# Moving the context stream's front and attention of the second block into the expert phase of layer 1, with a ring of four weight slots there

## The reference, cut to what matters

```
# first block, layer i
x = x + g1 * attention(h)
y = hierarchical_moe(h, ...)       # 32 experts: silu(h @ w_gate) * (h @ w_up), then @ w_down
x = x + g2 * y
# second block, layer l
hx = rmsnorm(x) * (1 + scale) + shift ;  hy = rmsnorm(y) * (1 + scale_c) + shift_c
fy, gy, qy, ky, vy, ay = branches(hy, ...)      # h @ w_in, Fourier mix, spatial gate, q, k, v
fx, gx, qx, kx, vx, ax = branches(hx, ...)
ox = attend(qx, [ky, kx], [vy, vx]) * silu(ax)
x = x + gate * (concat(fx, gx, ox) @ w_out)
if l < 1:
    oy = attend(qy, ky, vy) * silu(ay)
    y = y + gate_c * (concat(fy, gy, oy) @ w_out)
```

## Time and profile before

| | us |
|---|---|
| median of 3 runs | 1902.62 (1901.37 to 1910.19) |
| the profiled execution | 1905.12 |
| its span | 1903.3 |
| experts of layer 1 on TensorE | 974.98 to 1483.4 |
| y's front and attention between x's fills | 1507.52 to 1606.33 |

### The profile page before, as it was taken

How to read it: one execution, slowest core, us unless ns; L and a number is a source line. 1 busy time by engine, 2 the same in 40 slices (tenths; PEclk the granted TensorE clock), 3 DMA queues, 4 the chain that set the end, 5 groups by cost and what they waited for, 6 DMA issues and landing times.

```text
span 1903.3 us, 18238 instructions
## 1 busy us (share of the span) xinstructions
PE 1696.5 (89%) x7421; PEld 845.8 (44%) x7421; DVE 489.1 (26%) x927; ACT 405.1 (21%) x909; POOL 95.9 (5%) x167
## 2 busy tenths in 40 slices
PE   5967999888988888989989999989989899889988
PEld 3823453333333334835453433433343456555564
DVE  1337230000000103244241000000102344663362
ACT  2004221111111102015131111111100334443351
POOL 1102000000000010113000000000001000100000
PEclk9988999999999999989989999999999999999999
DMA  9997269999999999987369999999999622123310
GB/s 353 389 383 283 110 267 406 421 422 422 422 423 423 423 416 400 352 349 238 132 238 421 423 416 423 418 422 417 418 419 390 238 91 89 66 80 117 115 62 23
DMA packets 122520, 586.32 MB, mean 308 GB/s; under 512 B 10290, under 2 KB 15482, under 8 KB 97848
## 3 DMA queue, kind: packets, MB, share of 16 engines
q1 hardware_dynamic: 99064, 491.94, 64.0%
q0 software_dynamic: 16192, 82.06, 11.6%
q10 hardware_dynamic: 7168, 11.02, 1.5%
HBM read 572.83 MB, written 12.15 MB: 307 GB/s over the span
## 4 chain that ended last, share of the span: by engine, by line
PE 57%; DMA 28%; DVE 7%; ACT 4%; issue 3%; SPq 1%; ACTq 0%; DVEq 0%
PE psum L2025 53%; DMA ring<-in_expert_w_up 20%; DMA work<-in_ada_w 4%; DMA ring<-in_diff_w_in 2%; DVE work L1716 1%; DMA work<-in_ctx 1%; DMA ring<-in_consts 1%; PE psum L620 1%; DVE small L967 1%; PE psum L2264 1%; PE psum L1097 1%; DVE work L1924 1%; ACT work L1639 1%; SPq L499 0%; ACT work L1503 0%
## 5 line engine op out<-in xcount | busy, mean ns | idle before, releaser
L2025 PE MATMUL psum<-ring,work 128*64 128x512 f32 (+5 forms) x4432 | 1152.0, 576 | 77.1 <-DMA ring<-in_expert_w_up 60.2
L2025 PEld LDWEIGHTS psum<-ring,work 128*64 128x64 f32 (+2 forms) x4432 | 444.4, 153 | 700.8 <-issue 668.1
L2025 PE MATMUL psum<-work 128*128 128x192 f32 (+8 forms) x920 | 193.1, 377 | 9.1 <-DVE work L1862 5.0
L1924 DVE TENSOR_TENSOR work<-work,psum 128x256 f32<-128x256 f32 x64 | 26.9, 421 | 616.5 <-ACT work L1639 616.5
L2025 PEld LDWEIGHTS psum<-work 128*128 128x128 f32 (+2 forms) x920 | 131.7, 192 | 105.1 <-issue 85.2
L1639 ACT ACTIVATE work<-psum 128x256 f32<-128x256 f32 x64 | 24.5, 383 | 691.1 <-PE psum L2025 691.1
L2025 PE MATMUL psum<-work,ring 128*128 128x256 f32 (+1 forms) x728 | 159.5, 377 | 4.5 <-DMA ring<-in_diff_w_in 1.6
L2025 PEld LDWEIGHTS psum<-work,ring 128*128 128x128 f32 x728 | 134.8, 190 | 29.2 <-issue 7.1
L1503 ACT ACTIVATE work<-psum 128x256 f32<-128x256 f32 (+4 forms) x165 | 70.3, 439 | 220.0 <-PE psum L2025 67.7
L1946 DVE TENSOR_TENSOR work<-psum,rows 128x512 f32<-128x512 f32 x64 | 44.2, 691 | 272.1 <-PE psum L2025 272.1
L1716 DVE SCALAR_TENSOR_TENSOR work<-work,small 128x2048 f32<-128x2048 f32 x28 | 65.8, 2351 | 96.4 <-DMA work<-in_ada_w 96.0
(11 more groups left out here) (256 smaller groups left out, 813.7 us busy)
## 6 DMA issues: line engine op xcount, KB each, us to landing
ring<-in_expert_w_gate SPq DMA_DIRECT2D x60, 2048.0 KB, 16.7
ring<-in_expert_w_up SPq DMA_DIRECT2D x60, 2048.0 KB, 21.3
ring<-in_expert_w_down SPq DMA_DIRECT2D x57, 2048.0 KB, 21.1
work<-in_ada_w POOLq DMA_DIRECT2D x40, 1024.0 KB, 8.5
ring<-in_w_in SPq DMA_DIRECT2D x12, 2048.0 KB, 8.8
work<-in_w_mod POOLq DMA_DIRECT2D x16, 1024.0 KB, 5.2
ring<-in_diff_w_in SPq DMA_DIRECT2D x6, 2048.0 KB, 37.5
ring<-in_sb_w_in SPq DMA_DIRECT2D x6, 2048.0 KB, 24.6
```

The lines of the kernel that those rows point to most:

```text
L1924: V.tensor_tensor(hid, s_act, gu_bank(e)[:, S:2 * S], ALU.mult).then_inc(sem("hid"), 1)
L2025: return T.matmul(out_, lhsT, rhs, start=start, stop=stop, skip_group_check=True)
```

## The change

`Y0_AT` becomes (4, 5, 6, 7, 8): y's five sections run at five experts in a row, the turns at e = 2 and 3. From e = 9 on, `y0_step` runs the 15 front steps and the 20 attention steps of y inside the experts, two per expert: one before `gate_up` (half 0, odd steps), one before `turn(hid)` (half 1, even steps). `X0_IN` is gone. From expert 7's gate on (`SPLIT`), items go round four slots; slots 4 and 5 (`KEPT`) then hold the small weights, `cst2` and y's mix and v, which GpSimd loads on its queue during the experts. Tiles of y get rooms of their own (`space_y`), banks are given out anew in layer 1 (gate_up always in bank 0, down always in bank 5), and ScalarE loads the silu table again before each expert's silu where a y step has used another. x's scores over 512 keys are two matmuls of 256 columns where they were one of 512, since y's and x's keys lie apart.

```diff
@@ ring, tables
-    Y0_AT = (6, 11, 16, 21, 26)
+    Y0_AT = (4, 5, 6, 7, 8)
+    SPLIT_AT = 7
+    SPLIT = expert_item(1, SPLIT_AT, 0)
     def slot(n):
-        return n % RING
+        return n % RING if n < SPLIT else (n - SPLIT) % (RING - KEPT)
-    X0_IN = share_steps([0, 1, 1, 1, 1, 1, 2, 2, 2, 2, 2, 3, 3, 3, 3, 3, 1, 1, 1, 1])
+    FRONT, ATTN = 15, 20
+    Y0_STEP0 = Y0_AT[-1] + 1
+    def y0_step(front, attention, e, half):
+        j = 2 * (e - Y0_STEP0) + half - 1
+        if 0 <= j < FRONT:
+            front(0, j)
+        elif FRONT <= j < FRONT + ATTN:
+            attention(0, j - FRONT)
@@ SyncE and GpSimd
-            if r == 0:
-                small_weights(sp, 0, "small_in")
-                sp.dma_start(cst2, a["consts2"]).then_inc(sem("small_in"), 16)
+                for n in range(SPLIT - RING, SPLIT):
+                    if slot(n) >= RING - KEPT:
+                        pool.wait_ge(free(n), turn_of(n) + 1)
+                small_weights(pool, 0, "small_in")
+                pool.dma_start(cst2, a["consts2"]).then_inc(sem("small_in"), 16)
@@ ScalarE, experts
+                if l:
+                    y0_step(front, attention, e, 0)
+                    if y0_roots(e):
+                        act.preload_act_table(ACT.Silu)
                 act.wait_ge(sem("gu"), EACH["gu"] * l + e + 1)
...
                 if 0 < e < TAIL:
                     store(l, e - 1)
+                if l:
+                    y0_step(front, attention, e, 1)
@@ VectorE, experts
+                    y0_step(front, attention, e, 0)
                 dve.wait_ge(sem("silu"), EACH["silu"] * l + e + 1)
...
+                if l:
+                    y0_step(front, attention, e, 1)
...
-                V.tensor_tensor(outb[:, e % 2, :], bank[5 + e % 2], gate2, ALU.mult).then_inc(sem("out_ev"), 1)
+                V.tensor_tensor(outb[:, e % 2, :], bank[down_bank(l, e)], gate2, ALU.mult).then_inc(sem("out_ev"), 1)
@@ TensorE, second block
-        for n, js in enumerate(X0_IN):
+        for n in range(2 * len(fills(1))):
             in_half(1, n)
-            for j in js:
-                front(0, j) if j < FRONT else attention(0, j - FRONT)
@@ TensorE, attention step
-                mm(bank[4 + k % 3][:, 0:n * P], qT2[...], kT2[0:A_QK, hd, 0:n * P], True, True)
+                for j in range(1 + s):
+                    ins = mm(score_bank(p, k)[:, j * S:(j + 1) * S], space(p).q[...], kT2[j][0:A_QK, hd, :], True, True)
```

More of the change, by code:

```diff
@@ L14 @@
+from collections import namedtuple
 from contextlib import ExitStack
@@ L38 @@
 RING = 6
+KEPT = 2
 SLOT = KT * 512
@@ L261, in program @@
     ACC = (1, 3, 4, 7)
-    selw = work[:, 4416:5440].rearrange("p (e t k n) -> p e t k n", e=QUAD, t=TT, k=2)
+    GATHER = (3, 1)
+    selw = [t_.rearrange("p (e t k n) -> p e t k n", e=QUAD, t=TT, k=2) for t_ in (work[:, 4416:5440], rows[:, 2, :])]
     selT = work[:, hS_at:hS_at + 1024].rearrange("p (e t q) -> p e t q", e=QUAD, t=TT)
@@ L321, in down_done, with gu_bank, down_bank, turn_of @@
         down = expert_item(l, e, 2)
-        eng.wait_ge(*((sem("early_used"), EARLY[0] * l + e + 1) if e < EARLY[l] else (free(down), down // RING + 1)))
-    def gu_bank(e):
-        return bank[0 if e >= TAIL else e % 2]
+        eng.wait_ge(*((sem("early_used"), EARLY[0] * l + e + 1) if e < EARLY[l] else (free(down), turn_of(down) + 1)))
+    SPLIT_AT = 7
+    SPLIT = expert_item(1, SPLIT_AT, 0)
+    def gu_bank(l, e):
+        return bank[0 if l or e >= TAIL else e % 2]
+    def down_bank(l, e):
+        return 5 + (0 if l and e < TAIL else e % 2)
     def slot(n):
-        return n % RING
+        return n % RING if n < SPLIT else (n - SPLIT) % (RING - KEPT)
+    def turn_of(n):
+        return sum(slot(m) == slot(n) for m in range(n))
     def loaded(eng, n):
-        eng.wait_ge(sem(f"loaded{slot(n)}"), 16 * (n // RING + (slot(n) >= 4)))
+        eng.wait_ge(sem(f"loaded{slot(n)}"), 16 * (turn_of(n) + (slot(n) >= 4)))
     def free(n):
@@ L519, in sp_second @@
         last = expert_item(1, NX - 1, 2)
-        sp.wait_ge(free(last), last // RING + 1)
+        sp.wait_ge(free(last), turn_of(last) + 1)
         for r, (p, what) in enumerate(WEIGHTS2):
@@ L852, in act_second @@
         take_turned(act, copy, 1, range(KT), (2, 3, 4, 5))
-        for n, js in enumerate(X0_IN):
-            if n % 2:
-                take_fill(act, link, copy, 1, n // 2, n // 2 % 2)
-            for j in js:
-                front(0, j) if j < FRONT else attention(0, j - FRONT)
+        for n in range(len(fills(1))):
+            take_fill(act, link, copy, 1, n, n % 2)
         c_root(act, link, 1)
@@ L1000, in dve_second @@
             stream_diag(dve, link, 1, t)
-        c_norm(dve, link, 0)
-        v_norm(dve, link, 0)
-        for n, js in enumerate(X0_IN):
-            for j in js:
-                front(0, j) if j < FRONT else attention(0, j - FRONT)
-        attention(0, 19)
         c_squares(dve, link, 1)
@@ L1336, in overflow @@
             last = expert_item(l, TAIL - 1, 2)
-            for n in range(last - RING + 1, last + 1):
-                sp.wait_ge(free(n), n // RING + 1)
+            for n in range(last - RING + l * KEPT + 1, last + 1):
+                sp.wait_ge(free(n), turn_of(n) + 1)
             for e in range(NX):
@@ L1614, in experts @@
         def experts(l):
+            front, attention = act_steps(act, link, copy)[4:]
             act.preload_act_table(ACT.Silu)
@@ L2328, in experts @@
         def experts(l):
+            front, attention = pe_steps(pe, mm)[3:]
             for e in range(NX):
                 n0, q, i = expert_item(l, e, 0), e // QUAD, e % QUAD
-                if l and e in (3, 4):
-                    if e == 4:
+                if l and e in (2, 3):
+                    if e == 3:
                         pe.wait_ge(sem("h2T"), 2)
-                    turn_stream(pe, 0, range(4 * e - 12, 4 * e - 8), Y0_BANKS)
+                    turn_stream(pe, 0, range(4 * e - 8, 4 * e - 4), Y0_BANKS)
                 if l and e in Y0_AT:
```

274 lines of the change are left out of this document (171 added, 103 removed).

## The result

The changed kernel takes 1940.0 us (median of 4 runs, 1935.2 to 1944.3) against 1902.3 us before: 1.0189 times the time, with a 95% interval of 1.0154 to 1.0224. It is 38 us slower. The forecast was 1892.5 with 1877 to 1917, so the result lies above the range.

What follows compares the result with a forecast made beforehand. Transfers bound the experts, at 15.4 us each. Terms 28 + 7.7 + 3 + 1.5 - 50.3 = -10 us on the profiled 1905.1 give 1895; the median lies 2.5 lower: 1892.5 us, range 1877 to 1917.

Steps and rivals of the forecast that it cites:

- The transfers bind the experts: Layer 1's experts: DMA needs 15.4 us per expert, TensorE 12.63 us when nothing makes it wait, so DMA decides.
- Loss A: y's sections at experts 4 to 8: TensorE binds there, hid of expert 8 comes 51.5 us late, at 1147.3.
- The transfer-bound pace of 15.4: Experts 17 to 27: with attention steps TensorE needs 14.3 us, so hids come 15.4 us apart.
- The small loads cost nothing: GpSimd's 2.8 MB fall into the DMA stall during y's sections: cost 0; uncovered they would be 7 us.
- The second block: Its start: x's fills run in one stretch, output projection starts at 1556 instead of 1606.33, a gain of 50.3 us.
- The hand-offs fit: y's steps in the experts: ScalarE's part fits by half a microsecond; rival of missing it, 1900 or 1915, chance 0.15.
- Scores in two matmuls: x's two attentions, 32 steps: same columns but one weight load more, between 0 and 5 us, 1.5 taken.
- The ring of four: Four weight slots in the experts: next up lands barely in time, 3 us taken in all.
- The margin is nil: After up lands: the next up is needed by 10.4 us, work queued ahead of it takes 10.5 us.
- The ring starves itself: Experts 9 to 27: half-clock gate_ups and late landings feed each other, up to 32 us; typically 1909, chance 0.22.
- the clock should fall less often: Experts after e = 9: TensorE's waits shrink from 2.8 us to 1, so fewer half-clock gate_ups costing 1.7 us.
- The tail: Experts 29 to 31: waits for slots add 2.8, 3.3 and 1.6 us, +7.7 us together.

Runs made afterwards that it cites:

- y5_ring5: Kernel before with y's five sections at experts 4 to 8 and five slots from expert 7 on, no step moved: 1931.2 us, ratio 1.0144.
- y5_ring4: Kernel before with y's five sections at experts 4 to 8 and four slots from expert 7 on, no step moved: 1983.7 us, ratio 1.0402.
- y5: Kernel before with only y's five sections moved to experts 4 to 8, six slots kept: 1924.8 us, ratio 1.0104.
- warm: Changed kernel plus three unused matmuls of 256 columns ahead of gate_up's wait in experts 11 to 29: 1937.4 us, ratio 1.0166.
- halves: Changed kernel, items from expert 9 loaded as two 1 MB parts, each slot part freed early, gate_up starting on first parts: 1891.4 us, again 1893.0 us.
- late: Changed kernel, from expert 10 to 29 SyncE issues the next expert's down only after the turn of hid: 1935.2 us, ratio 1.0164.

## Why the prediction was wrong

**What held.** The transfers bind the experts: yes. Loss A: `hid` of expert 8 at 1147.3 forecast, 1147.2 measured. The transfer-bound pace of 15.4 is what y5_ring5 shows, with its five slots. The small loads cost nothing: GpSimd's last one (704 KB) is issued at 1119.85 and lands 14.3 us later, at 1134.2, while TensorE first needs c at 1162.8, and the DMA engines stood at a share of 0.12 from 1105 to 1115. The second block: -50.3 forecast, -50.0 measured. The hand-offs fit: TensorE waits 1.4 us in all for ScalarE and VectorE in the experts, so that rival is out. Scores in two matmuls: the end of the traces is 36.8 us apart (1940.1 against 1903.3) and the output projection's start 32.5, of which 1.7 are its start at half clock (`turn_c` follows 34.2 us later than before, from 1616.74 to 1650.89). The remaining 2.6 us (36.8 less 34.2) hold this term, for which 1.5 was taken; it wasn't tried by itself.

**Where it failed.** The step is "The ring of four", and in it "The margin is nil ... I take 3 us in all". By the prediction's own count the term is 38 to 40 us: from `hid` 8 to 27 y5_ring4 takes 330.6 us where 19 x 15.4 are 292.6, and the changed kernel 336.3 where the prediction had 296.2, without the 3. That is 2.0 to 2.1 us per expert, mis-sized thirteenfold. (Against y5 it is 45.7 us, because the prediction's count has none of what six full slots give y5.)

Two readings in that step were wrong. The first is "Queued ahead of it are down and the next gate, 2 x 5.0, and the store 0.47: 10.5", counted from the landing of up. The windows of y5_ring4 and warm show 8.7 and 7.3 us of work left at that moment, since part of what stands behind up has moved before up lands. The next up is issued just as this is through. Second, what lies outside the bytes "costs 0", as it would "overlap partly with the queue". It can't where the queue has run out. How a load begins on an empty queue shows in the kernel before, in one that has the engines to itself (w_out, issued at 1706.38, landed at 1714.41):

```profile
core 0: us, PE busy (x) PEld busy (x) DVE busy (x) ACT busy (x) POOL busy (x), PEclk, DMA share, GB/s
1706.38:1707.38 1.00, 1.00 (x3) 0.38 (x2) 0.63 (x2) 0.98 (x2) 0.00 (x0) 1.00 0.00 0
1707.38:1709.00 1.62, 1.62 (x5) 0.76 (x4) 0.22 (x1) 0.91 (x2) 0.00 (x0) 1.00 0.89 205
1709.00:1713.50 4.50, 4.21 (x10) 1.52 (x8) 0.15 (x1) 0.00 (x0) 0.00 (x0) 1.00 1.02 389
1713.50:1714.41 0.91, 0.00 (x0) 0.00 (x0) 0.88 (x2) 0.00 (x0) 0.00 (x0) 1.00 0.05 16
```

Nothing moves for 1.0 us, and then 205 GB/s for 1.6 us, which loses another 0.8: together 1.8 us at the start, the size of the gap in warm. Of the 3.0 us outside the bytes only the 0.9 after the last byte leave the engines free for other loads. So each turn pays about 2 us in which the engines are idle or slow, and nineteen experts pay it. I had put the whole risk on half-clock gate_ups, which cost 1.7 each. What stays open is what sets the time of a landing in the loop: an up that is issued 1.7 us earlier lands no earlier.

**The rival had the outcome but not the mechanism.** "The ring starves itself" gave at most 32 us, and by the clock: half-clock gate_ups that feed themselves. Warm took the half-clock gate_ups away from 1300 to 1440 and the pace stayed, 17.9 against 18.1. A gate_up at half clock does widen the gap in its turn (20.7 us from 1391.07 to 1411.74), but it isn't why turns are too long. The argument against it, that y's steps fill TensorE's gaps, and the expectation that "the clock should fall less often" were wrong: from 1241 to 1473 nine of the fourteen gate_ups in the changed kernel's chain take 8.48 to 10.08 us, and the granted clock is 0.92 from 1274 to 1474, where it was 0.98 before in the earlier trace rows. The steps help a little (0.89 without them, in y5_ring4), but the pace did not hang on it.

**The tail.** +7.7 was forecast from expert 27 to the end of the experts, +14.7 measured, in the changed kernel and within 0.5 in y5_ring4 (73.6 against 73.9 us from `hid` 27 to 31, where it was 59.2). The queue runs dry in it too: no byte moves from 1522 to 1525, while the pieces of expert 30 wait for the end of gate_up 29. In halves the same stretch takes 66.1, +6.9, near the forecast. In all, x's first fill comes 82.5 us later where 28 + 3 + 7.7 = 38.7 was forecast.

**With the ring's term gone, the sum holds.** In halves, which keeps four slots, the experts at 27 are 27.4 us late (28.6 counted from expert 0) where 28 was forecast, and the time is 1891 to 1893 where 1892.5 was. What was wrong is in the main this one term, and with it the range, whose upper end of 1917 left out the full case of the ring. The tail's other 7 us go with it, since halves gives them back too.

**The Trainium skill.** DMA: Bandwidth & Descriptors, Anatomy of one DMA, gives about 2.0 us fixed for a transfer; the figure is fitted on transfers that GpSimd issues, and the page puts most of it behind the last byte. The load at 1706.38, which SyncE issued, does not bear this out: 3.0 us lie outside its bytes, and only 0.9 of them behind the last one. That the 1.8 us at the start are near 2.0 is no agreement. And the conclusion that I drew from the page in the prediction, that the term would then be 0, was wrong by the same 38 to 40 us.

## What to carry to other kernels

Before slots are given to something else, follow one slot through a turn: when it comes free, when its next item lands, when that is used. Here up was issued when gate_up ended, and the next gate_up waited for it, so a turn was at least gate_up's 7.1 us, a load's 8.0 and the issue's 0.3: 15.4, just what the bytes need, with nothing to spare for the other loads that share the engines meanwhile. A fifth slot took up out of this loop and was enough. If the margin of a queue is nil, every turn pays the start of a transfer (here 1.8 us), so multiply it by the number of turns. And what is queued behind an item does not wait for it to land: count what is left at its landing in a window of the trace. When slots are short, load an item in halves and start on the first: that gave the time back here without a byte of memory.

## What was not expected of the hardware

- The landing took longer just where the item was issued earlier: 8.3 to 8.9 us after a gate_up that began at half clock, 9.8 to 10.6 after one at full clock in the changed kernel's chain from 1213 on, with the turn near 17.5 in most. With down issued 1.7 us after up (late) both stayed so. How the engines share two loads queued one behind the other stays open.
- Transfers of 1 MB instead of 2 MB, with nothing else changed, moved 387 GB/s instead of 367 in the same starved loop (pace 17.1 for 18.1). Why smaller ones leave a smaller gap was not taken apart.
